# Layer-one mixer: the state scan placed ahead of a weight split, the gated output's split among the bias masks, and half products from attention's first step

## The reference, cut to what matters

```python
def hybrid_layer(h, ...):
    u = rmsnorm(h, norm_mix_pre)
    proj = u @ w_in                      # q, k, v of attention; q, k, v, gate of the linear attention
    o_na = rmsnorm(neighbourhood_attention(q_na, k_na, v_na, rpb), na_gain)
    o_gl = gla_bidirectional(q_gl, k_gl, v_gl, g_gl, z_gl, ...)
    mix = jnp.concatenate([o_na, o_gl], axis=-1) @ w_o
    h = h + rmsnorm(mix, norm_mix_post)
    ...                                  # then a gated feed-forward network

def gla_chunked(q, k, v, log_a, strict):
    ...
    _, s_prev = lax.scan(step, s0, (decay, ds))   # step: dec[..., None] * s + d
    return o + jnp.einsum('bhncd,nbhde->bhnce', q_dec, s_prev)

# gla_bidirectional ends in: o = rmsnorm(o, out_gain) * silu(g)
```

## Time and profile before

| | |
|---|---|
| median of 3 runs | 1958.05 us (1955.08 to 1962.77) |
| profiled execution | 1958.58 us, its span 1956.8 us |
| PE busy | 1784.4 us, 91% of the span |
| PE weight load busy | 1532.5 us, 78% |
| DVE busy | 1021.0 us, 52% |
| ACT busy | 650.2 us, 33% |
| POOL busy | 88.5 us, 5% |
| mean granted clock of PE | 0.958 of full speed |

### The profile page before, as it was taken

How to read it: one execution, slowest core, us unless ns; L and a number is a source line. 1 busy time by engine, 2 the same in 40 slices (tenths; PEclk the granted TensorE clock), 3 DMA queues, 4 the chain that set the end, 5 groups by cost and what they waited for, 6 DMA issues and landing times. The chain is left out here.

```text
span 1956.8 us, 38581 instructions
## 1 busy us (share of the span) xinstructions
PE 1784.4 (91%) x17168; PEld 1532.5 (78%) x17168; DVE 1021.0 (52%) x1524; ACT 650.2 (33%) x1060; POOL 88.5 (5%) x115
## 2 busy tenths in 40 slices
PE   6998789978999999988999998888669999999998
PEld 5888667877998989878777777677558888878877
DVE  3246564435663654554665355655556545353554
ACT  3242233433442332343333334333144322121232
POOL 6000000010000000010000000000001100000020
PEclk8999987988999999989999999999979999999999
DMA  5211130030222222221212100000052222222221
GB/s 160 87 66 44 55 108 1 1 109 32 99 87 106 88 87 87 89 100 65 76 65 103 70 34 4 4 5 10 3 204 87 90 104 87 108 86 97 97 87 65
DMA packets 29132, 144.57 MB, mean 74 GB/s; under 512 B 6315, under 2 KB 9659, under 8 KB 14380
## 3 DMA queue, kind: packets, MB, share of 16 engines
q1 hardware_dynamic: 24828, 133.58, 19.1%
q0 software_dynamic: 3856, 7.87, 1.3%
q10 hardware_dynamic: 288, 0.73, 0.1%
HBM read 134.82 MB, written 8.91 MB: 73 GB/s over the span
## 5 line engine op out<-in xcount | busy, mean ns | idle before, releaser
L228 DVE TENSOR_TENSOR w_w_lo<-w_w_raw,w_w_hi 128x2048 fp32r<-128x2048 f32 x67 | 153.5, 2292 | 192.7 <-ACT w_w_hi L215 192.4
L240 PE MATMUL f_bank<-u_hi,w_w_hi 128*128 128x258 f32 x704 | 203.5, 289 | 12.3 <-DVE w_w_lo L228 6.2
L241 PE MATMUL f_bank<-u_hi,w_w_lo 128*128 128x258 f32 x704 | 202.3, 287 | 0.0
L242 PE MATMUL f_bank<-u_lo,w_w_hi 128*128 128x258 f32 x704 | 200.9, 285 | 0.0
L240 PE MATMUL g_bank<-g_y_hi,g_w_hi 128*128 128x512 f32 x384 | 151.1, 394 | 16.5 <-DVE g_w_lo L228 12.2
L242 PE MATMUL g_bank<-g_y_lo,g_w_hi 128*128 128x512 f32 x384 | 150.3, 391 | 0.0
L241 PE MATMUL g_bank<-g_y_hi,g_w_lo 128*128 128x512 f32 x384 | 150.2, 391 | 0.0
L240 PEld LDWEIGHTS f_bank<-u_hi,w_w_hi 128*128 128x128 f32 x704 | 135.3, 192 | 13.7 <-DVE w_w_lo L228 6.4
L215 ACT ACTIVATE g_w_hi<-g_w_raw 128x2048 fp32r<-128x2048 f32 x45 | 85.9, 1908 | 166.9 <-PE g_bank L242 165.3
L215 ACT ACTIVATE w_w_hi<-w_w_raw 128x2048 fp32r<-128x2048 f32 x67 | 127.6, 1904 | 32.0 <-PE f_bank L242 32.0
L242 PEld LDWEIGHTS f_bank<-u_lo,w_w_hi 128*128 128x128 f32 x704 | 136.1, 193 | 0.0
(11 more groups left out here) (509 smaller groups left out, 3980.0 us busy)
## 6 DMA issues: line engine op xcount, KB each, us to landing
g_w_raw<-in_w_ff SPq DMA_DIRECT2D x32, 1024.0 KB, 4.7
w_w_raw<-in_w_in SPq DMA_DIRECT2D x30, 1024.0 KB, 4.8
w_w_raw<-in_w_ffn_in SPq DMA_DIRECT2D x22, 1024.0 KB, 4.8
w_w_raw<-in_w_ffn_out SPq DMA_DIRECT2D x12, 1024.0 KB, 4.8
w_w_raw<-in_w_o SPq DMA_DIRECT2D x4, 1024.0 KB, 5.1
gate_pre<-rw_t POOLq DMA_DIRECT2D x16, 256.0 KB, 2.3
g_w_raw<-in_w_up SPq DMA_DIRECT2D x4, 1024.0 KB, 8.8
g_branch<-gate_pre SPq DMA_DIRECT2D x4, 1024.0 KB, 11.9
```

Source lines behind the costliest of these rows:

```text
L228: nc.vector.tensor_tensor(R.lo[:, r, 0:size], R.raw[:, r, 0:size], R.hi[:, r, 0:size].bitcast(F32), ALU.subtract).then_inc(R.split, 1)
L240: nc.tensor.matmul(out, w_hi, u_hi, start=start, stop=False)
L241: nc.tensor.matmul(out, w_lo, u_hi, start=False, stop=False)
L242: return nc.tensor.matmul(out, w_hi, u_lo, start=False, stop=stop)
```

## The change

1. DVE does the 28 scan instructions first, and the weight split `split_more(("scan", 0))` after them.
2. In the norm part, ACT takes GLA's square roots first and the meta softmax's Exp after them; DVE sums and scales that softmax after the 20 multiplications instead of between them.
3. The split of GLA's gated output (L968, L1208) goes to memory of its own, `mix_hi_u` (over rows 0 to 3 of `h`) and `mix_lo_u` (over `gla_in`), and its five pieces stand among the first five bias masks. A new buffer `spare` and free columns of `vg` take the kept parts.
4. The meta softmax's transposes go in front of mask 6, its products into attention's step 0.
5. Half products go in from step 0: 12 in step 0, 6 in steps 1 to 26 (every fourth step has all 6 in the third place), 2, 2, 2, 4, 2 in steps 27 to 31, and the last 12 behind attention. `w_o`'s second slot for GLA is split in four pieces on each engine (ACT in steps 1 to 4, DVE in steps 5 to 8) instead of in one.
6. A one-column Sqrt (`warm`) stands on ACT behind the last step's copy, ahead of the last two outputs. The last kept part comes behind the square roots.
7. SP's reload of `h` waits for the last half product as well.

```diff
+        mix_hi_u = nc.alloc_sbuf_tensor_at("m_mix_hi", [P, 4, L], F32R, offset=h_place)
+        mix_lo_u = nc.alloc_sbuf_tensor_at("m_mix_lo", [P, 4, L], F32R, offset=gla_place)
...
-        FIRST = 7
-        per_step = lambda i: ((0, 3, 3), (3, 3, 3), (3, 3, 3))[(i - FIRST) % 3] if FIRST <= i < FIRST + 24 else (0, 0, 0)
+        opening_steps = [(3, 6, 3), (2, 2, 2), (2, 2, 2)]
+        steady = [(0, 0, 6), (2, 2, 2), (2, 2, 2), (2, 2, 2)]
+        closing = [(0, 0, 2)] * 3 + [(0, 2, 2), (0, 0, 2)]
+        per_step = opening_steps + 6 * steady + closing
...
             sp.wait_ge(o_done, NI)
+            sp.wait_ge(R.tile_done, wo_gla.end())
             sp.dma_start(h[:], io["h"]).then_inc(h_back, 16)
...
             for hh in range(NA_H):
                 if hh:
                     pe.wait_ge(masked, hh)
+                if hh == 6:
+                    pe.wait_ge(ms, 6)
+                    pe.wait_ge(mix_lo2, 5)
+                    for head in range(NA_H):
+                        last = nc.tensor.transpose(bank[0:META, 1, head * META:head * META + META], sm[:, head, :],
+                                                   eye[0:META, 0:META])
+                    last.then_inc(mt_done, 1)
...
                     if g == 0:
                         pe.wait_ge(mix_lo2, 5)
-                        pe.wait_ge(mo_read, 1)
-                    else:
-                        pe.wait_ge(R.tile_free, wo_gla.c0 + g)
+                    pe.wait_ge(R.tile_free, wo_gla.c0 + g)
...
+                if i == 1:
+                    pe.wait_ge(mo_read, 1)
...
+                if i == 0:
+                    pe.wait_ge(mt_copied, 1)
+                    pe.wait_ge(R.tile_free, tm_na.end())
+                    for hh in range(NA_H):
+                        last = nc.tensor.matmul(bank[0:META, 3, hh * 64:hh * 64 + 64], pm[:, hh * META:hh * META + META],
+                                                vg[0:META, 4, hh * 64:hh * 64 + 64], start=True, stop=True)
+                    last.then_inc(mo_done, 1)
...
             values(NI - 1)
+            for _ in half_gemm:
+                pass
...
-            act.wait_ge(ms, 3)
-            nc.scalar.activation(sm[:], sm[:], ACT.Exp).then_inc(mp_done, 1)
             act.wait_ge(osq_sum, 5)
             for nn, tt in ((P, slice(0, 4)), (META, slice(4, 5))):
                 nc.scalar.activation(ssq[0:nn, tt, :], ssq[0:nn, tt, :], ACT.Sqrt, scale=1.0 / GLA_DV, bias=EPS).then_inc(g_std, 1)
+            act.wait_ge(ms, 3)
+            nc.scalar.activation(sm[:], sm[:], ACT.Exp).then_inc(mp_done, 1)
             evacuate(("norm", 0))
             for hh in range(NA_H):
+                if hh < 5:
+                    act.wait_ge(ot2, hh + 1)
+                    nc.scalar.activation(mix_hi_u[:, :, tok[hh]], out_bank(hh), ACT.Copy, scale=gain("gla_gain")).then_inc(mix_hi2, 1)
                 evacuate(("masks", hh))
...
+                if 1 <= i <= 4:
+                    hi_piece(wo_gla.n0 + 1, i - 1, tm_na.end())
...
             copy_ptm(NI - 1)
+            nc.scalar.activation(warm, C("ones")[:, 0:1], ACT.Sqrt)
             read_o(NI - 2)
...
+            keep_part(KT - 1)
...
-            split_more(("scan", 0))
             dve.wait_ge(ds_read, NCK)
             dve.wait_ge(qk, QK * 5)
             for step in range(1, NCH):
...
+            split_more(("scan", 0))
...
                 last.then_inc(masked, 1)
+                if hh < 5:
+                    dve.wait_ge(mix_hi2, hh + 1)
+                    nc.vector.scalar_tensor_tensor(mix_lo_u[:, :, tok[hh]], out_bank(hh), gain("gla_gain"),
+                                                   mix_hi_u[:, :, tok[hh]].bitcast(F32), ALU.mult, ALU.subtract).then_inc(mix_lo2, 1)
                 split_more(("masks", hh))
...
-                if i == 1:
-                    ahead_lo(dve, nc, R, wo_gla.n0 + 1)
+                if 5 <= i <= 8:
+                    lo_piece(wo_gla.n0 + 1, i - 5)
```

More of the change, by code:

```diff
@@ L395, in mixer_block @@
         pt = tmp[:].rearrange("p a b -> p (a b)")[:, 0:6 * P].rearrange("p (a b) -> p a b", a=2)
-        om = gla_in[0:META, 4, 0:512]
+        om = vg[0:META, 0:4, 1040:1040 + P]
         near_v = h[:, 4:8, 0:512]
-        scratch = vg[:, 4, 1024:1536]
-        part = lambda m: vg[:, m, 512:512 + L] if m < 4 else gla_in[:, m - 4, :]
+        scratch = gla_in[:, 4, 0:512]
+        parts = [vg[:, m, 512:512 + L] for m in range(4)] + [spare[:, 0, :], spare[:, 1, :], vg[:, 4, L:2 * L], gla_in[:, 4, :]]
+        part = lambda m: parts[m]
         nm, den, rden = st[:, 0:2], st[:, 2:34], st[:, 34:66]
-        ss, nrs = st[:, 66:71], st[:, 71:76]
+        ss, nrs, warm = st[:, 66:71], st[:, 71:76], st[:, 92:93]
         mmx, msum = st[0:META, 76:84], st[0:META, 84:92]
@@ L743, in half_products @@
                         pe.wait_ge(mix_lo2, 5)
[L744 to L746 removed]
+                    pe.wait_ge(R.tile_free, wo_gla.c0 + g)
                     for k in range(4):
                         c0 = 1024 * (m // 2) + k * SLOT + (m % 2) * P
[L749 to L750 removed]
+                        for left, right in ((R.hi, mix_hi_u), (R.lo, mix_hi_u), (R.hi, mix_lo_u)):
+                            start, stop = k == 0 and left is R.hi and right is mix_hi_u, k == 3 and right is mix_lo_u
                             for i in range(2):
[L752 removed]
+                                last = nc.tensor.matmul(bank[:, 6 + i, 0:HALF], left[:, r, c0:c0 + P], right[:, k, halves[i]],
                                                         start=start, stop=stop)
@@ L812, in _ @@
             for i in range(NI):
-                run_half(per_step(i)[0])
+                run_half(per_step[i][0])
                 if i + 1 < NI:
                     scores(i + 1)
-                run_half(per_step(i)[1])
+                if i == 0:
[5 more added lines that the diff above has]
+                    last.then_inc(mo_done, 1)
+                run_half(per_step[i][1])
                 turn(i)
-                run_half(per_step(i)[2])
+                run_half(per_step[i][2])
                 if i >= 1:
                     values(i - 1)
[L821 to L832, removed]
             values(NI - 1)
+            for _ in half_gemm:
+                pass
             pe.wait_ge(o_read, NI)
@@ L961, in _ @@
                 nc.scalar.activation(ssq[0:nn, tt, :], ssq[0:nn, tt, :], ACT.Sqrt, scale=1.0 / GLA_DV, bias=EPS).then_inc(g_std, 1)
+            act.wait_ge(ms, 3)
+            nc.scalar.activation(sm[:], sm[:], ACT.Exp).then_inc(mp_done, 1)
             evacuate(("norm", 0))
             for hh in range(NA_H):
+                if hh < 5:
+                    act.wait_ge(ot2, hh + 1)
+                    nc.scalar.activation(mix_hi_u[:, :, tok[hh]], out_bank(hh), ACT.Copy, scale=gain("gla_gain")).then_inc(mix_hi2, 1)
                 evacuate(("masks", hh))
+                if hh == 6:
+                    act.wait_ge(mt_done, 1)
+                    nc.scalar.activation(pm[:], bank[0:META, 1, 0:P], ACT.Copy).then_inc(mt_copied, 1)
             evacuate(("last", 0))
-            for t in range(5):
-                act.wait_ge(ot2, t + 1)
-                nc.scalar.activation(u_hi[:, 4:8, tok[t]], out_bank(t), ACT.Copy, scale=gain("gla_gain")).then_inc(mix_hi2, 1)
-            ahead_hi(act, nc, R, wo_gla.n0 + 1, tm_na.end())
             def read_o(i):
```

30 lines of the change are left out of this document (13 added, 17 removed).

## The result

| | before | changed |
|---|---|---|
| median of 3 runs | 1958.05 us | 1932.10 us (1930.56 to 1939.23) |
| ratio | | 0.9864, 95% interval 0.9841 to 0.9886 |
| profiled execution, its span | 1958.58, 1956.8 us | 1930.56, 1928.8 us |
| mean granted clock | 0.958 | 0.967 |

The time lies in the range (1919 to 1941), 6 us above the 1926 forecast. By the profiled executions 28.0 us were gained where the sum said 32.0. The gain inside the mixer was larger than the sum, and part of it was gone again some 30 us later. (The FFN in the table is the feed-forward network that follows the mixer.)

The account below looks back on a forecast made before the run. The prediction took the stretch to be PE-bound, partly at half clock, with four waits. Terms 9.2 + 1.6 + 2.9 - 0.4 + 17.9 + 0.8 = 32.0 off 1958.58 gave 1926.6, forecast as 1926 us, range 1919 to 1941.

Parts of the forecast that it names:

- the sum: All terms of the change together: 32.0 us gained, taken from the profiled execution of 1958.58.
- Scan, 9.2: State products: scan ahead of the weight split removes PE's 7.7 us wait and about 1.5 at low clock.
- Norm, 1.6: Norm part: square roots come 1.95 us earlier, so DVE starts the masks 1.6 earlier; bounds 0.5 to 1.95.
- Split among the masks, wait ahead of the scores, 2.9 - 0.4: Masks to first scores: split pieces cost 0, PE's wait shrinks by 2.9 us, meta transposes lose 0.4.
- the cover: First five masks: DVE's 1.00 us idle in each hides a 0.6 us split piece; cost 0, bounds 0 to 0.6.
- Attention, 17.9: Attention shrinks from 112.2 to 94.3 us, mostly by steps 0 to 9 running at full clock.
- Both conditions: Attention: the clock holds with about 6 fillers a step, and no other engine becomes the bound.
- my sign: Attention: prediction wrong if a stretch shows 0.50, or PE waits for ACT or DVE over some tenths a step.
- Behind attention, 0.8: Behind attention: the 1.28 us table load moves ahead of two outputs, pushing the last by up to 0.45; 0.8 gained.
- Rival "clock kept behind attention": Behind attention: PE's shorter pause keeps the clock up, 2 to 5 us more gained, 1922; chance 0.13.
- what bounds the kernel now: Prediction's opening part: the stretch from 203 to 412 us is PE-bound, partly at half clock, with four waits.

Follow-up runs that it names:

- e5_split_behind: Changed kernel with the gated output's split and the meta softmax's transposes put back behind the masks; 1942.16 us, ratio 0.991.
- e9_before_filler: Kernel before with 15 matmuls that nobody reads added in PE's pause ahead of the FFN's first weight slot; 1963.47 us, ratio 1.0019.
- e10_before_again: Kernel before, unedited, one more execution for its trace; 1959.73 us.
- e1_after: Changed kernel run again without an edit; 1933.91 us, ratio 0.9857 to the kernel before.
- e4_late_fill: Changed kernel with the half products back in the steps where the kernel before had them, from step 7; 1945.60 us, ratio 0.9931.
- e6_no_table_ahead: Changed kernel without the one-column Sqrt ahead of the last outputs; 1934.40 us, ratio 0.9866.
- e11_after_again: Changed kernel, unedited, one more execution for a third trace; 1930.96 us.
- e3_scan_undone: Changed kernel with the weight split put back in front of the scan; 1945.89 us, ratio 0.9921.

## Why the prediction was nearly right, and the step that failed

*Scan, 9.2.* Right in kind: wait and slow group are gone. The state products came 8.61 sooner where 7.7 was said (the scan began at 211.33, not 212.2, and PE's filler too ended 0.9 sooner), and with the 1.45 of clock behind them it is 10.1. That 8.61 is in part the luck of the two traces: the clock also falls between 201 and 218 us, ahead of the state products, in twelve of the fourteen traces, and in neither of these two. The state products start between 222.25 and 228.65 in the ten traces with the scan first, and between 230.86 and 236.29 in the four without. Taken back alone it costs 12.0, done alone it gives 12 to 14, in both cases more than the sum of the rows; what the surplus is stays open.

*Norm, 1.6.* The roots came 236.92 - 235.61 = 1.31 behind the end of the last square (3.25 before), so 1.94 sooner for the 1.95 that was forecast. From state products to the first flip it took 21.58 for 24.48; 2.90 less, of which 1.45 is the clock's part of the scan's term. What is left is 1.45.

*Split among the masks, wait ahead of the scores, 2.9 - 0.4.* From the first flip to the first scores 3.09 less. The masks where a piece lies take 2.2 us each with DVE still idle 0.35 ahead of them: the cover held. e5_split_behind gives 4.1 for the wait alone.

*Attention, 17.9.* 112.2 became 95.2, 17.0 less (93.7 in seven later traces), forecast 94.3. The length was right; the 17.9 leaned on a long first trace, since the attention of before took 109.3 in e9_before_filler and e10_before_again, which makes the gain 15.6. Steps 2.59, 3.13, 3.23 for 2.5, 3.1, 3.2. Both conditions held: PE idled 0.4 us in the 73 that e1_after shows, and the clock stayed at 1.00 but for one dip of 3.4 us at 0.50 in the first trace. By the letter of my sign (wrong if a stretch in attention shows 0.50) that dip speaks against me; it cost 1.5 us and didn't come again. The reason is also right, in two parts: without the filler the clock falls though no pause stands ahead (e4_late_fill, 11.6 us), and with the pause it falls though the filler is there, and comes back under it (e5_split_behind, 6.2 us).

*Behind attention, 0.8.* 0.98 by the marks, 0.99 by e6_no_table_ahead. The Trainium skill (ScalarE: Activation LUTs, section What ACT_TABLE_LOAD costs) has 2.66 us for a switch, and my estimate from it was 2.2 here. The trace of e6_no_table_ahead agrees with its 1.28 for the load but has 0.02 us ahead of the load and 0.01 behind it, so no room for the drain that the Trainium skill adds, and the measurement decides.

*Rival "clock kept behind attention".* In part: 9.46 became 8.47 from the diagonal products to the projection, and 27.35 became 26.08 from there to the first L320, 2.3 us in all, and there the clock fell again at 363.0, at 373.2 and at 400.5. In e1_after it is 7.19 and 26.06, 3.6 us, and in e11_after_again, where the clock stayed at 1.00 from 210 to 404, 7.19 and 24.55, 5.0 us. So the rival that I left out of the forecast came true in part, and for the total it made up some of what slot 0 lost: that the time lies near the forecast is to that extent luck.

Up to the first L320 the mixer thus gave 34.77 for 32.0, and 34.71 in the second pair of traces, with less in attention and more behind it.

*The failed step* is the sentence that closes "what bounds the kernel now": **"After it the feed-forward network starts from this chain's end, and what is saved here should be saved at the end."** The sum lacks a term for what stands behind the mixer: -6.1 us in the FFN's first slot. It is 30.1 to 30.3 long in the three traces of the changed kernel, in e3_scan_undone and in e4_late_fill, 24.2 in the three traces with the attention of the kernel before, and 28.4 in e5_split_behind and e6_no_table_ahead. In the kernel before, that slot also began at the low clock, so its length depended on when the clock came back, and I took that length as fixed. Then, by the kernel before's times, 1.3 came back in the second slot, 1.5 went until 861 us, 3.3 until 930 (1.7 where the changed kernel has 20.5 us at 0.50 and the other 17, and 1.5 in a fall at 857.9 to 861.3 that the other hasn't), and 3.3 came back between 1057 and 1391: 34.8 - 6.1 + 1.3 - 1.5 - 3.3 + 3.3 = 28.5, and half a us less at the end.

What stays open: why the clock comes back behind one group in the kernel before and behind four in the changed one. The wait ahead of it and the instructions are the same. The ten traces without added products ahead of slot 0 lean to the moment of arrival. In all of them the clock fell between PE's first L320 and the end of the products behind it (L329), ahead of the wait of 3.79. From that fall to slot 0's first product it is 7.31 to 7.35 us in the three traces in which the slot takes 24.2, 7.46 to 7.60 in four of the five with 30.1 to 30.3 (4.43 in e11_after_again), and 4.84 and 4.85 in the two with 28.4. One of these two, e6_no_table_ahead, has the changed kernel's slot and all its work ahead of it but for one table load's place, so the work alone doesn't decide it. But this sorts ten traces and proves nothing: no run delayed the changed kernel there by a chosen time.

## What to carry to other kernels

Where an engine is busy at the low clock, look at what its instructions are and not for a wait: large products put among small ones can be worth more than their own time, here some 10 us of attention (11.6 less 1.4) for spreading the 192 instructions from the first step on. Work saved ahead of a place where the clock is low isn't all saved at the end: list each such place behind the change, and put a range on it, here up to 6 us. Take more than one trace of the kernel before: its attention took 112.2 in one and 109.3 in two. A few products that nobody reads in a wait of 2 to 4 us can fix that (6.5 us for fifteen), but only a timing of the whole tells: the same fifteen made the kernel before 3.8 us slower.

## What the hardware showed that I had not expected

The clock falls under full load: 20.00 of 20.00 us busy at 0.50 with transposes and values of 128 columns and 64-row scores (e4_late_fill), and it stays low under 15.97 of 16.00 in slot 0, where groups of 12 products alternate with 12 one-column sums. The Trainium skill (TensorE: Matmul & The Clock Gate, Part 1: The HAM clock gate) has the clock follow how busy the array has lately been; by the profile's busy time neither stretch should be at the low clock, so busy time isn't the measure of it here. Slot 0's stretch holds no transposes, so these can't be the whole reason; no run told transposes, 64-row scores and one-column sums apart. The Trainium skill's other half on that page, that idle time lowers the clock, agrees with the fall in or right behind the pauses of 7.72 and 3.13 in the kernel before and of 4.08 in e5_split_behind. Behind 2.51 us ahead of the diagonal products it fell in the first trace of the changed kernel and not in the next two, and ahead of slot 0 it had fallen before the long wait.
